# A fused two-block kernel: the delta rule's inverse in 64 by 64 products, the weights' high half first, and a new merged order

## The chip, the cores and the metric

One core of one Trainium2 chip. The metric is the device time of one execution in microseconds (us). The kernel is written instruction by instruction for the five engines: TensorE (PE, its weight loads shown as PEld), VectorE (DVE), ScalarE (ACT), GpSimd (POOL) and SyncE (SP), which only issues transfers.

## The reference, cut to what matters

There are 256 tokens of width 1024. Block one, two layers, mixes sparse attention with a gated delta rule. Block two, two layers, mixes four kinds of attention. All weights are float32 and are read once.

The part that the change rewrites is the delta rule's chunk solve. There are 8 heads, chunks of 64 tokens, and each chunk has a unit lower triangular matrix of 64 by 64:

```python
lower = jnp.where(strict, jnp.einsum('bhnid,bhnjd->bhnij', kb, k) * decay, 0.0)
tmat = jnp.eye(CHUNK) + lower
u = lax.linalg.triangular_solve(tmat, v * beta[..., None], left_side=True, lower=True, unit_diagonal=True)
w = lax.linalg.triangular_solve(tmat, kb * jnp.exp(gc)[..., None], left_side=True, lower=True, unit_diagonal=True)
```

The rest of the work is projections `h @ w_in`, `mixed @ w_out` and their likes in block two, and the attentions.

## The kernel before, in words

**Projections ("mm" steps).** The weights come as 277 units of up to 128 by 1024 float32. SP loads a unit into one of five raw slots. ACT copies it to a float32r high half (step `split`, L1345 by way of L1331). POOL subtracts to get the low half (L849). PE then multiplies in three passes, high by high, high by low, low by high (L916; L902 for the tiles whose stationary operand is the weights; L909 for the narrow ones). Before the first matmul of a unit, PE waits for POOL's low half. Most units are 12 instructions of 512 columns each or 24 of 256.

**The delta rule.** The kernel works on 128 tokens at once (row block r = 0, 1), on four heads at a time (group g = 0, 1), in two layers: four inverses in all. A 128 by 128 lower triangular matrix is inverted: 8 by 8 diagonal blocks first, on DVE (`sub`), then four levels that double the block, 8, 16, 32, 64. `x1` turns the start on PE with transposes. A level n has: `invY`, four products lt by xx on PE (L1014), masked by DVE into yy (L1996); `invZ`, four products xt by yy on PE (L1014), subtracted by DVE from xx (L2003); `invT`, four PE transposes of xx (L937), copied by ACT into xt. The last level is done on the 64-row halves (L1059, L1061 are its two interleaved products; each reads 64 rows and writes 128 partitions). A four-product step is 8 PE instructions (two for each float32 product); a four-transpose step is 4.

**Attention scores on 64-row operands.** `raw` (L1124), `sbz` (L1212) and `sc2` (L1272) hold two heads in the two 64-row halves of a tile. Their loops do the products of the lower rows first, then those of the upper rows.

**Order.** Every engine runs its own instructions in order. The steps come from lanes (a: chains of the delta rule and the like, b: attention, s: splits, m: mm, c, d, v, w: convolution and drains, x, y, e: the ends of layers), and one string, ORDER, says letter by letter which lane goes next. All engines follow this one merged order, so PE does a chain step and then an mm unit and so on, and a chain's latency on DVE and ACT lies behind mm units. Two PSUM tiles of 4 KB a partition ("chain") are taken in turn by chain steps; two others ("bulk") by the projections.

In the merged order of before, PE's steps around the inverse of layer 1, group 0, read (g.r.n): x10.0 x10.1 invY0.0.0 invY0.1.0 invZ0.0.0 invZ0.1.0 vT0 invY0.0.1 mm26 invT0.0.0 invY0.1.1 invT0.1.0 mm27 mm28 iT0 invZ0.0.1 invZ0.1.1 invY0.0.2 invT0.0.1 mm29 and so on.

Of the kernel before, what the change touches and what calls it, by code (L numbers as in the profile page):

```python
# [25 lines left out]
ALU = mybir.AluOpType  # L26
# [3 lines left out]
P = 128  # L30
S = 256
# [22 lines left out]
K_ID, K_TRIU, K_LEVEL, K_BLOCK, K_NEG, K_STR, K_NSTR, K_TRIL, K_ONE, K_FREQ, K_UNIT, K_LATER, K_HALF = (  # L54
    0, 128, 256, 768, 896, 1152, 1408, 1664, 1792, 1920, 1960, 1968, 2096)
K_COLS = K_HALF + 1


def shape_constants():
# [5 lines left out]
    for n, s in enumerate(LEVELS):  # L65
        c[:, K_LEVEL + n * P:K_LEVEL + (n + 1) * P] = (
            (p // (2 * s) == f // (2 * s)) & (p // s % 2 == 1) & (f // s % 2 == 0))
    c[:, K_BLOCK:K_BLOCK + P] = p // BLK == f // BLK
    c[:, K_UNIT:K_UNIT + BLK] = p % BLK == np.arange(BLK)[None, :]
# [162 lines left out]
def gdn_chain(g):  # L232
# [3 lines left out]
    for n in range(len(LEVELS)):  # L236
        for r in range(R):
            if n < len(LEVELS) - 1 or not r:
                out.append(("invY", g, r, n))
            if n:  # L240
                out.append(("invT", g, r, n - 1))
# [59 lines left out]
def lanes():  # L301
# [20 lines left out]
    "aaaaasamsmvasmsmasassasmaaaacmamscsccascmmsaccaasmmcssmasammcscscmmaasdasbamabmasamsaammmsasabsmmaas"  # L322
    "dmaamcsbaaaasmaaasaadmsaasmasdmaaaasaaamaabamaamssacbmsamsacsmcamsbscacsmcmsbascmmcbcmscsascambmbmab"
    "sbaasmsasaaamabdassmmbsmmsmacmdabsdsmaasmaamaawassbdbabmsmamaxmsxsbbbmwamabsabxbasamasaaasbaababamaa"
    "dsdsbamawswmsmbsammamabsdsaamsmwsxdaxmasxxxbswsmxxbbxammsxsvssmvsmmaaaasmmsssmmmamamsvdmaasmassmssmm"
    "acaacmssmccscamcsacsmamsmcsasaccmmmsamsassacamamascsaamsdammssmmammmadssaabsaasbaaaamabsaamdmsbaasaa"
    "maabadaaaaamaaabsssmabmabamaamcsscascmscsabcmmascmmscsbcmcmsscasmcmabmabsaasdmsaaasbmaasbmasmmsdbmam"
    "sambmscamasssaaaaaamdbsaawmxsasmbbbamsdbmbmabssamaxbbmbbsmssdbbmwwammsabasdaaamsxaamdwaawamamsxsabsm"
    "sasbxsamadawbabxxmxmxsssxmxxsmsvsmsmvsmmsamaammaasasmassammmsmsmdsmmssdsabsmmsmdssdssmmbmmmasmsbasas"
    "amamsbbdadammmabssabsdmbmbabbvamsassdabbmasmbsambbssmmbddasbmdmsbbsmbsbsymamyabdysmsabdvmasbyysmdbds"  # L330
    "yysvvdssdmmymsvvvvmmmmmssvmmdvvvvssymsmsmvvsssyvvsmmvvmsmmmemsmemsmsevvmvvaeamesmmeaamsmmmssmmassmms"
    "dmmsssdmsmbdmamssbaasssadasbamsmammmmbabbdsbbsmsammbbdsabamdabbmbavmssbasmbsabmbymsdmbasmbdsdssaambb"
    "mmbasmyysbdsdmssayvmbsmdydbymyvvssmdysmmsvvmdssssvvvmmmdvvsmmsvvysvvsmmsmymssmvvmmsvvemmeemvvmvvmmme"
    "ee"
# [3 lines left out]
def plan():  # L338
# [17 lines left out]
    "kk": "vector", "rep": "vector", "x1": "scalar", "kT": "vector", "invY": "vector", "invZ": "vector", "invT": "scalar", "vT": "vector",  # L356
# [105 lines left out]
def build(nc, t, out):  # L462
    ctx = ExitStack()
    with ctx:
# [62 lines left out]
        kd, st = xx[:, 0, :, :], xx[:, 1, :, :]  # L527
        xt = area(R, 4, P)
        yy = area(R, 4, P)
        rhs = xx[:, 0, :, :].rearrange("p j n -> p (j n)")  # L530
# [160 lines left out]
        def bank_order(i, per):  # L691

            return 2 * (i % (per // 2)) + i // (per // 2)

# [162 lines left out]
        def _(pe):  # L857
            def handlers(p):
# [15 lines left out]
                def mm(u, half=None):  # L874
# [16 lines left out]
                    pe.wait_ge(*p.after("gpsimd", "split", u))  # L891
# [3 lines left out]
                    for k in range(nk):  # L895
                        kk = k0 + k
                        if w["lhs"] == "T":
                            for j in range(4):
                                dst = pair[:, j * S:(j + 1) * S]
                                a_hi, a_lo = hi[:, k, j * P:(j + 1) * P], lo[:, k, j * P:(j + 1) * P]  # L900
                                for i, (a, b) in enumerate(((a_hi, hT_hi), (a_hi, hT_lo), (a_lo, hT_hi))):
                                    m = pe.matmul(dst, a, b[:, kk, :], start=(kk == 0 and i == 0 and j % 2 == 0),  # L902
                                                  stop=(kk == tot - 1 and i == 2 and j % 2 == 1),
                                                  skip_group_check=True)
                        elif w["lhs"] == "narrow":
                            if p.sec == "one" and kk % 4 == 0:
                                pe.wait_ge(*p.after("vector", "hT", kk // 4))
                            for i, (a, b) in enumerate(((hi, hT_hi), (hi, hT_lo), (lo, hT_hi))):
                                m = pe.matmul(pair[0:n, 0:S], a[:, k, :], b[:, kk, :], start=(kk == 0 and i == 0),  # L909
                                              stop=(kk == tot - 1 and i == 2))  # L910
                        else:
                            for r in range(R) if half is None else (half,):
                                dst = pair[:, r * 512:r * 512 + n]
                                a_hi, a_lo = lhs(w, kk, r)
                                for i, (a, b) in enumerate(((a_hi, hi), (a_hi, lo), (a_lo, hi))):
                                    m = pe.matmul(dst, a, b[:, k, :], start=(first and k == 0 and i == 0),  # L916
                                                  stop=(last and k == nk - 1 and i == 2))
# [16 lines left out]
                def transposes(c, srcs, n=P):  # L934

                    for i, v in enumerate(srcs):
                        m = pe.transpose(c[0:n, i * P:i * P + v.shape[0]], v, ident[0:v.shape[0], 0:v.shape[0]])  # L937
                    return m
# [105 lines left out]
                def invY(g, r, n):  # L1044
# [3 lines left out]
                    else:  # L1048
                        pe.wait_ge(*p.after("vector", "invZ", g, r, n - 1))
                    if n < len(LEVELS) - 1:  # L1050
                        four(c, [(lt[:, r, j, :], xx[:, r, j, :]) for j in range(4)]).then_inc(p.done("invY"), 1)
                    elif r == 0:
                        four(c, [(lt[0:P // 2, r, j, :], xx[0:P // 2, r, j, :]) for j in range(4)]).then_inc(p.done("invY"), 1)
                    else:
                        pe.wait_ge(*p.after("vector", "invY", g, 0, n))
                        pe.wait_ge(*p.after("scalar", "invT", g, 0, n - 1))
                        low, up = slice(0, P // 2), slice(P // 2, P)
                        for j in range(4):
                            pe.matmul(c[:, j * P:(j + 1) * P], yy[up, 0, j, :], xt[up, 0, j, :], start=(j == 0), stop=(j == 3),  # L1059
                                      skip_group_check=True)  # L1060
# [1393 lines left out]
```

## Time and profile before

| | us |
|---|---|
| runs | 1102.52, 1100.67, 1099.73 |
| median | 1100.67 |
| profiled execution, first to last instruction (span) | 1099.5 |
| PE busy | 1057.8 (96% of the span) |
| POOL / DVE / ACT busy | 661.4 / 633.4 / 589.4 |
| mean granted TensorE clock | 0.992 |

Three runs stand beside one profiled execution, for which the span is the only time given. "Busy" is time in which an engine has at least one instruction in flight; a matmul's shown duration includes the pipeline's latency, so the cost of a matmul in a stream is the distance from its start to the next one's start, not its duration.

### The profile page before, as it was taken

What the parts mean: (1) busy time and instruction counts of PE and PEld (TensorE: products, weight loads), DVE (VectorE), ACT (ScalarE), POOL (GpSimd) and SP (SyncE); (2) the same over time, 40 slices, a digit from 0 to 9 for tenths busy, and PEclk for the clock granted to TensorE, in tenths of its full rate; (3) what the DMA queues carried; (4) which work ended last, traced back from release to release, by engine and by line L of the source; (5) the groups of instructions that cost most, each with busy time, mean ns of one, the idle gap of its engine ahead of it and who ended that gap; (6) DMA issues with size and microseconds to landing.
All of it is one profiled execution on the core that took longest, in us unless ns stands there. A gap on an engine that the chain in (4) does not pass through costs nothing.

```text
span 1099.5 us, 16938 instructions
## 1 busy us (share of the span) xinstructions
PE 1057.8 (96%) x6368; PEld 916.2 (83%) x6368; DVE 633.4 (58%) x1193; ACT 589.4 (54%) x994; POOL 661.4 (60%) x286
## 2 busy tenths in 40 slices
PE   8999999999989999999999998999999899999986
PEld 8988898888877998889888887788888677898865
DVE  4777358786475547547578465506436650655564
ACT  3753347554644485336756644355577534557652
POOL 4775455854546777525755554697454877645493
PEclk9999999999999999999999998999999999999998
DMA  8644334434234555314444333474332556433361
GB/s 284 205 154 134 97 116 135 154 116 153 96 98 127 190 167 161 118 56 136 141 147 134 97 116 96 137 244 143 116 106 86 194 151 210 129 94 117 110 200 49
DMA packets 80575, 151.60 MB, mean 138 GB/s; under 512 B 6448, under 2 KB 12400, under 8 KB 80496
## 3 DMA queue, kind: packets, MB, share of 16 engines
q1 hardware_dynamic: 80496, 150.54, 42.9%
q8 instruction: 51, 0.84, 0.3%
q14 instruction: 28, 0.23, 0.1%
HBM read 149.47 MB, written 1.05 MB: 137 GB/s over the span
## 4 chain that ended last, share of the span: by engine, by line
PE 84%; DVE 6%; ACT 3%; POOL 3%; issue 3%; DMA 0%; POOLq 0%; SPq 0%; DVEq 0%; ACTq 0%
PE bulk L916 49%; PE bulk L902 11%; PE chain L1014 8%; PE chain L937 6%; POOL w_lo L849 2%; PE chain L1291 1%; PE chain L1272 1%; PE chain L1144 1%; PE bulk L909 1%; PE chain L1160 1%; ACT w_hi L1331 1%; DVE arena L1730 1%; ACT arena L1331 1%; PE chain L1005 1%; PE chain L1124 1%
## 5 line engine op out<-in xcount | busy, mean ns | idle before, releaser
L849 POOL TENSOR_TENSOR w_lo<-raw,w_hi 128x1024 fp32r<-128x1024 f32 (+4 forms) x277 | 647.0, 2349 | 416.7 <-ACT w_hi L1331 416.1
L1331 ACT ACTIVATE w_hi<-raw 128x1024 fp32r<-128x1024 f32 (+4 forms) x277 | 279.5, 1019 | 187.3 <-PE bulk L916 157.8
L916 PE MATMUL bulk<-w_hi,hT_hi 128*128 128x512 f32 (+1 forms) x756 | 307.0, 406 | 10.4 <-POOL w_lo L849 5.8
L916 PE MATMUL bulk<-w_hi,hT_lo 128*128 128x512 f32 (+1 forms) x756 | 295.3, 391 | 0.0
L916 PE MATMUL bulk<-w_lo,hT_hi 128*128 128x512 f32 (+1 forms) x756 | 295.0, 390 | 0.0
L916 PEld LDWEIGHTS bulk<-w_hi,hT_hi 128*128 128x128 f32 x756 | 142.9, 189 | 44.9 <-issue 10.1
L916 PEld LDWEIGHTS bulk<-w_hi,hT_lo 128*128 128x128 f32 x756 | 142.6, 189 | 29.9
L916 PEld LDWEIGHTS bulk<-w_lo,hT_hi 128*128 128x128 f32 x756 | 143.0, 189 | 26.0 <-issue 1.0
L1331 ACT ACTIVATE arena<-chain 128x512 f32<-128x512 f32 (+4 forms) x92 | 62.0, 686 | 118.1 <-PE chain L937 88.5
L902 PE MATMUL bulk<-hT_hi,w_hi 128*128 128x256 f32 x384 | 111.2, 290 | 0.0
L902 PE MATMUL bulk<-hT_hi,w_lo 128*128 128x256 f32 x384 | 108.7, 283 | 0.0
L902 PE MATMUL bulk<-hT_lo,w_hi 128*128 128x256 f32 x384 | 108.6, 283 | 0.0
L1014 PE MATMUL chain<-arena 128*128 128x128 f32 (+1 forms) x800 | 105.3, 279 | 3.0 <-DVE arena L2003 0.8
L1014 PEld LDWEIGHTS chain<-arena 128*128 128x128 f32 (+1 forms) x800 | 98.1, 191 | 10.8 <-DVE arena L2003 1.9
L937 PE MATMUL chain<-cst,arena 128*128 128x128 f32 (+3 forms) x672 | 92.5, 275 | 3.9 <-DVE sT_lo L1675 1.4
L937 PEld LDWEIGHTS chain<-cst,arena 128*128 128x128 f32 (+3 forms) x672 | 76.8, 141 | 15.1 <-DVE sT_lo L1675 1.6
L902 PEld LDWEIGHTS bulk<-hT_hi,w_hi 128*128 128x128 f32 x384 | 73.6, 192 | 1.2 <-issue 0.8
L1838 DVE SCALAR_TENSOR_TENSOR arena<-bulk,par,arena 128x253 f32<-128x253 f32 (+2 forms) x144 | 59.4, 474 | 25.8 <-ACT arena L1331 24.5
L902 PEld LDWEIGHTS bulk<-hT_lo,w_hi 128*128 128x128 f32 x384 | 73.6, 192 | 0.0
L902 PEld LDWEIGHTS bulk<-hT_hi,w_lo 128*128 128x128 f32 x384 | 73.5, 191 | 0.0
L1331 ACT ACTIVATE arena<-bulk 128x1024 f32<-128x1024 f32 (+2 forms) x50 | 50.3, 1006 | 35.3 <-PE bulk L916 35.1
L1326 ACT ACT_TABLE_LOAD x40 | 51.3, 1283 | 24.5 <-PE bulk L916 8.1
(259 smaller groups left out, 1331.4 us busy)
## 6 DMA issues: line engine op xcount, KB each, us to landing
raw<-in_w_in_dram SPq DMA_DIRECT2D x194, 512.0 KB, 3.4
raw<-in_w_out_dram SPq DMA_DIRECT2D x32, 512.0 KB, 3.5
raw<-in_w_branch_dram SPq DMA_DIRECT2D x16, 512.0 KB, 3.6
raw<-in_w_mem_kv_dram SPq DMA_DIRECT2D x8, 512.0 KB, 3.7
raw<-in_w_merge_up_dram SPq DMA_DIRECT2D x16, 256.0 KB, 2.7
raw<-in_w_in_dram SPq DMA_DIRECT2D x8, 420.0 KB, 3.2
gain<-in_ln_rows_dram SPq DMA_DIRECT2D x4, 512.0 KB, 5.1
gain<-in_gains_dram SPq DMA_DIRECT2D x3, 512.0 KB, 5.9
```

Of the source, the lines that this page charges most:

```text
L849: pool.tensor_tensor(lo_of(p, u)[:, 0:n], raw_of(p, u)[:, 0:n], hi_of(p, u)[:, 0:n].bitcast(F32), ALU.subtract).then_inc(p.done("split"), 1)
L902: m = pe.matmul(dst, a, b[:, kk, :], start=(kk == 0 and i == 0 and j % 2 == 0), stop=(kk == tot - 1 and i == 2 and j % 2 == 1), skip_group ...
L909: m = pe.matmul(pair[0:n, 0:S], a[:, k, :], b[:, kk, :], start=(kk == 0 and i == 0), stop=(kk == tot - 1 and i == 2))
L916: m = pe.matmul(dst, a, b[:, k, :], start=(first and k == 0 and i == 0), stop=(last and k == nk - 1 and i == 2))
L937: m = pe.transpose(c[0:n, i * P:i * P + v.shape[0]], v, ident[0:v.shape[0], 0:v.shape[0]])
L1005: pe.matmul(c[:, j * P:(j + 1) * P], spread(4 * g + j, 8), gcT[:, r * P:(r + 1) * P], start=(j == 0), stop=(j == 3), skip_group_check=True)
L1014: m = pe.matmul(c[:, j * P:(j + 1) * P], a, b, start=(j == 0), stop=(j == 3), skip_group_check=True)
L1124: m = pe.matmul(c[:, i * nk:(i + 1) * nk], qiT[lo_:lo_ + 64, h // 2, qb * P:(qb + 1) * P], kiT[lo_:lo_ + 64, 0:nk], start=(i * nk % 512 == 0),
L1144: m = pe.matmul(c[:, j * nk:(j + 1) * nk], qaT[:, 4 * kv + j, qb * P:(qb + 1) * P], kaT[:, kv, 0:nk], start=(j * nk % 512 == 0), stop=((j ...
L1326: act.preload_act_table_set(sets[func])
L1331: return act.activation(dst, src, func, **more)
L1838: ins = STT(cv[:, j, back:S], b[:, j * S:(j + 1) * S - back], par1[:, p.l, c:c + 1], cv[:, j, back:S], ALU.mult, ALU.add)
```

## The change

Five parts.

1. The inverse works on compact halves. The two 64 by 64 diagonal blocks of a 128 by 128 matrix stand in partitions 0 to 63 and 64 to 127 of a tile of 64 columns. A level is now products of 64 rows by 64 columns by 64 columns, two to a head, one in each diagonal quadrant, alternating (`half_blocks`). `invZ` makes both Z and its transpose (operands swapped) in one step, so `invT` is gone from PE and ACT; DVE subtracts both, each of 128 by 256 elements where it subtracted one of 128 by 512. `x1` becomes products with the identity. The last level writes only the 64 partitions that it needs.
2. An mm unit does all passes that need the weights' high half first, waiting only for ACT; then it waits for POOL and does the passes of the low half. The instructions are the same in number and shape.
3. `raw`, `sbz`, `sc2` take their products in the order 0, n/2, 1, n/2+1, ..., so lower-row and upper-row products alternate (`bank_turns`).
4. ORDER is new, without the 24 `invT` steps. Around the inverse of layer 1, group 0, PE's steps now read: x10.0 x10.1 mm24 invY0.0.0 mm25 invY0.1.0 invZ0.0.0 invZ0.1.0 mm26 vT0 invY0.0.1 mm27 iT0 iT1 mm28 invY0.1.1 invZ0.0.1 invZ0.1.1 invY0.0.2 invY0.1.2 invZ0.0.2 invZ0.1.2 invY0.0.3 mm29 invY0.1.3 kT0 mm30 invZ0.1.3.
5. The level masks in the constants are 64 columns wide, and the constants 1841 columns, from 2097.

```diff
+        xh, yh, xth = xx[:, :, :, 0:HALF], yy[:, :, :, 0:HALF], yy[:, :, :, HALF:P]
...
+        def bank_turns(per):
+
+            return [i for pair in zip(range(per // 2), range(per // 2, per)) for i in pair]
...
-                    pe.wait_ge(*p.after("gpsimd", "split", u))
...
+                    pe.wait_ge(*p.after("scalar", "split", u))
+                    for low in (False, True):
+                        if low:
+                            pe.wait_ge(*p.after("gpsimd", "split", u))
+                        part = lo if low else hi
+                        for k in range(nk):
...
+                                for r in range(R) if half is None else (half,):
+                                    dst = pair[:, r * 512:r * 512 + n]
+                                    a_hi, a_lo = lhs(w, kk, r)
+                                    for i, a in enumerate((a_hi,) if low else (a_hi, a_lo)):
+                                        m = pe.matmul(dst, a, part[:, k, :], start=(first and not low and k == 0 and i == 0),
+                                                      stop=(last and low and k == nk - 1))
...
+                def half_blocks(c, pair, col=0):
+
+                    for j in range(4):
+                        for at in halves:
+                            a, b = pair(j, at)
+                            m = pe.matmul(c[at, col + j * HALF:col + (j + 1) * HALF], a, b, start=(j == 0), stop=(j == 3),
+                                          skip_group_check=True)
+                    return m
...
-                    transposes(c, [xt[:, r, j, :] for j in range(4)]).then_inc(p.done("x1"), 1)
+                    half_blocks(c, lambda j, at: (xth[at, r, j, :], ident[at, at])).then_inc(p.done("x1"), 1)
...
-                        four(c, [(lt[:, r, j, :], xx[:, r, j, :]) for j in range(4)]).then_inc(p.done("invY"), 1)
+                        half_blocks(c, lambda j, at: (lt[at, r, j, at], xh[at, r, j, :])).then_inc(p.done("invY"), 1)
...
-                        four(c, [(xt[:, r, j, :], yy[:, r, j, :]) for j in range(4)]).then_inc(p.done("invZ"), 1)
+                        half_blocks(c, lambda j, at: (xth[at, r, j, :], yh[at, r, j, :]))
+                        half_blocks(c, lambda j, at: (yh[at, r, j, :], xth[at, r, j, :]), 512).then_inc(p.done("invZ"), 1)
...
-                def invT(g, r, n):
-                    c = take("invT", g, r, n)
-                    pe.wait_ge(*p.after("vector", "invZ", g, r, n))
-                    transposes(c, [xx[:, r, j, :] for j in range(4)]).then_inc(p.done("invT"), 1)
...
-                    for i in range(per):
+                    for i in bank_turns(per):
```

## Rows read from the trace of the kernel before

**Rows 1.** The page: PE's busy time, and the chain that ended last.
```profile
PE 1057.8 (96%) x6368; PEld 916.2 (83%) x6368; DVE 633.4 (58%) x1193; ACT 589.4 (54%) x994; POOL 661.4 (60%) x286
...
PE 84%; DVE 6%; ACT 3%; POOL 3%; issue 3%; DMA 0%; POOLq 0%; SPq 0%; DVEq 0%; ACTq 0%
PE bulk L916 49%; PE bulk L902 11%; PE chain L1014 8%; PE chain L937 6%; POOL w_lo L849 2%; PE chain L1291 1%; PE chain L1272 1%; PE chain L1144 1%; PE bulk L909 1%; PE chain L1160 1%; ACT w_hi L1331 1%; DVE arena L1730 1%; ACT arena L1331 1%; PE chain L1005 1%; PE chain L1124 1%
```

**Rows 2.** Waits of PE: total us, times, longest.
```profile
PE bulk L916 <- POOL w_lo L849: 7.6, 11, 1.8
PE bulk L916 <- issue: 5.7, 3, 3.6
...
PE bulk L909 <- POOL w_lo L849: 0.4, 1, 0.4
```

**Rows 3.** Busy time by window: start:end and length, PE, PEld, DVE, ACT, POOL, clock, DMA.
```profile
600.00:708.00 108.00, 101.65 (x565) 86.43 (x563) 59.75 (x92) 53.84 (x99) 57.33 (x23) 0.97 0.37 117
```

**Rows 4.** Groups of PE instructions by line: busy us, mean ns.
```profile
L1014 PE MATMUL chain<-arena 128*128 128x128 f32 (+1 forms) x800 | 105.3, 279 | 3.0 <-DVE arena L2003 0.8 <-DVE arena L1996 0.8 <-DVE arena L2023 0.7
L937 PE MATMUL chain<-cst,arena 128*128 128x128 f32 (+3 forms) x672 | 92.5, 275 | 3.9 <-DVE sT_lo L1675 1.4 <-DVE arena L1992 0.8 <-DVE arena L1996 0.4
```

**Rows 5.** The chain that ended last, in order of time: start us, length us.
```profile
96.53 1.79 PE chain L1014 x16
98.31 2.79 PE bulk L916 x12
...
116.30 0.44 PE chain L937 x4
```

**Rows 6.** Timeline of PE, 127.5 to 129.5 us: start us, length us.
```profile
127.53 0.66 PE L937 MATMUL chain<-cst,arena 128*128 128x128 f32 x4 [0.27 <-DVE arena L1992]
128.11 0.37 PE L1059 MATMUL chain<-arena 64*128 64x128 f32 x1
128.12 0.37 PE L1061 MATMUL chain<-arena 64*128 64x128 f32 x1
128.33 0.27 PE L1059 MATMUL chain<-arena 64*128 64x128 f32 x1
...
129.21 0.39 PE L902 MATMUL bulk<-hT_hi,w_hi 128*128 128x256 f32 x1
129.43 0.28 PE L902 MATMUL bulk<-hT_lo,w_hi 128*128 128x256 f32 x1
```

**Rows 7.** Weight loads of 8 and of 128 columns: min/median/max ns.
```profile
L987 PEld LDWEIGHTS chain<-cst,tiny x8: 87/90/91, 34.2 to 392.6; 128*8 128x8 f32 x8
...
L971 PEld LDWEIGHTS chain<-tiny,cst x8: 186/192/193, 30.3 to 383.2; 128*128 128x128 f32 x8
```

**Rows 8.** Timeline of PE at 802 us: 64 moving columns, 128 weight columns.
```profile
802.00 1.00 PE L1291 MATMUL chain<-arena 128*128 128x64 f32 x8
802.84 1.04 PE L937 MATMUL chain<-cst,arena 128*128 128x128 f32 x8
```

**Rows 9.** Timeline of weight loads after an idle wait of PE, 65.5 us.
```profile
65.55 0.18 PEld L1005 LDWEIGHTS chain<-cw_rows,cst 8*128 8x128 f32 x1 [0.80 <-issue]
65.59 0.18 PEld L1007 LDWEIGHTS chain<-arena,cst 8*128 8x128 f32 x1
```

**Rows 10.** DVE and ACT instructions around the inverse: min/median/max ns.
```profile
L1996 DVE TENSOR_TENSOR arena<-chain,cst x24: 690/692/693, 98.1 to 627.0; 128x512 f32<-128x512 f32 x24
...
L1331 ACT ACTIVATE arena<-chain x92: 267/597/1028, 65.2 to 1033.2; 128x512 f32<-128x512 f32 x58, 128x1024 f32<-128x1024 f32 x22, 8x128 f32<-8x128 f32 x4, 128x128 f32<-128x128 f32 x4
```

**Rows 11.** Timeline of PE: the steps raw, 16 and 8 instructions.
```profile
143.96 1.71 PE L1124 MATMUL chain<-arena 64*128 64x128 f32 x16
145.60 0.39 PE L902 MATMUL bulk<-hT_hi,w_hi 128*128 128x256 f32 x1
...
159.96 1.14 PE L1124 MATMUL chain<-arena 64*128 64x256 f32 x8
```

**Rows 12.** POOL's low half of the weights: min/median/max ns.
```profile
L849 POOL TENSOR_TENSOR w_lo<-raw,w_hi x277: 1012/2396/3382, 13.2 to 1080.3; 128x1024 fp32r<-128x1024 f32 x124, 128x512 fp32r<-128x512 f32 x8, 128x840 fp32r<-128x840 f32 x4, 128x704 fp32r<-128x704 f32 x1
```

More of the change, by code:

```diff
@@ L239, in gdn_chain @@
                 out.append(("invY", g, r, n))
-            if n:
-                out.append(("invT", g, r, n - 1))
         if n == len(LEVELS) - 1:
@@ L327 @@
[L327 to L331, printed above, removed]
@@ L894, in mm @@
                     lo = lo_of(p, u)[:, 0:nk * n].rearrange("p (k n) -> p k n", k=nk)
[L895 to L917, printed above, removed]
@@ new lines, in mm @@
+                    pe.wait_ge(*p.after("scalar", "split", u))
[4 more added lines that the diff above has]
+                        for k in range(nk):
+                            kk = k0 + k
+                            if w["lhs"] == "T":
+                                for j in range(4):
+                                    dst = pair[:, j * S:(j + 1) * S]
+                                    for i, b in enumerate((hT_hi,) if low else (hT_hi, hT_lo)):
+                                        m = pe.matmul(dst, part[:, k, j * P:(j + 1) * P], b[:, kk, :],
+                                                      start=(not low and kk == 0 and i == 0 and j % 2 == 0),
+                                                      stop=(low and kk == tot - 1 and j % 2 == 1),
+                                                      skip_group_check=True)
+                            elif w["lhs"] == "narrow":
+                                if p.sec == "one" and kk % 4 == 0 and not low:
+                                    pe.wait_ge(*p.after("vector", "hT", kk // 4))
+                                for i, b in enumerate((hT_hi,) if low else (hT_hi, hT_lo)):
+                                    m = pe.matmul(pair[0:n, 0:S], part[:, k, :], b[:, kk, :], start=(not low and kk == 0 and i == 0),
+                                                  stop=(low and kk == tot - 1))
+                            else:
+                                for r in range(R) if half is None else (half,):
[4 more added lines that the diff above has]
+                                                      stop=(last and low and k == nk - 1))
@@ L1209, in sbz @@
                     n = S - k * P
-                    for q in range(4):
+                    for q in bank_turns(4):
                         h = head_of(1, q)
@@ L1269, in sc2 @@
                     nk = keys_of(n, qb)
-                    for q in range(4):
+                    for q in bank_turns(4):
                         h = head_of(n, q)
@@ L1309, in handlers @@
                             p2T=p2T, pv2=pv2, yT=yT, gT=gT, mm=mm, memT=memT, hT=hT, cwT=cwT, gc=gc_, stat=stat, gcT=gcT_, avT=avT_, dec=dec, kk=kk, rep=rep, x1=x1, kT=kT, vT=vT,
-                            invY=invY, invZ=invZ, invT=invT, kq=kq, u=u_, st=st_, ks=ks, o=o_, iT=iT, raw=raw_, qT=qT, kaT=kaT_,
+                            invY=invY, invZ=invZ, kq=kq, u=u_, st=st_, ks=ks, o=o_, iT=iT, raw=raw_, qT=qT, kaT=kaT_,
                             sc=sc, pT=pT, pv=pv, mT=mT)
```

102 lines of the change are left out of this document (57 added, 45 removed).

## The prediction

> **What bounds the kernel now.** I read the page first [rows 1]: PE is busy for 1057.8 of 1099.5 us, and the chain that ended last lies on PE for 84%. The waits of PE [rows 2] are small and spread; the clock [rows 3] falls only where a layer ends, and there PE idles 6 us of 108. So the time is the sum of what PE has to do plus some 40 us of idle time, and an edit counts by the PE time that it takes away, unless it opens a wait. DVE, ACT and POOL are busy for under 61%; work taken from them counts only through PE's waits.
>
> Durations on PE include latency, so I cost by start-to-start distance. Two L1014 steps, 16 instructions, last 1.79 us and an mm unit 2.79 [rows 5]: 0.112 us for one of the two instructions of a float32 product of 128 by 128 by 128. Four transposes take 0.44, 0.109 each [rows 5].
>
> **Part 1, the inverse: what goes.** For one layer and group, x1 has 8 transposes; invY and invZ at three levels and two row blocks have 96 instructions; invT has 24 transposes; the last level has 8, 16 interleaved and 8. That is 32 x 0.109 = 3.5, 96 x 0.112 = 10.8, and for the last level 0.9 + 0.9 + 0.9 = 2.7 us, since the 16 interleaved run as 8 pairs, both of a pair within 0.01 us, 0.112 a pair [rows 6]. Sum 16.9, and 67.7 us for the four inverses. It is all on PE's path (448 of the 800 and 128 of the 672 instructions of [rows 4]; the rest of them stay; L1059 and L1061 hold 64 more).
>
> **What comes.** Each half_blocks call is 16 instructions, 8 pairs. There are 20 calls (x1 2, invY 6, invZ 12), and the last level has 8 single, 8 pairs, 8 single: 184 places for one layer and group, 736 in all. The unknown is the time p of a place with 64 weight columns and 64 moving ones. Bounds:
> - Low, 0.056. A weight load of 8 columns shows 90 ns and one of 128 shows 192 [rows 7], so 64 columns cost about 0.054 less than 128; half of 0.112 is 0.056. 736 places are 41.2 us.
> - High with pairing, 0.112: L1291 moves only 64 columns under 128 weight columns, and its 8 instructions still take 0.84 to the next start and so give no gain [rows 8]. I read that as the weight load being the limit, which the change halves too; were it not, 736 places are 82.4 us.
> - Between: after an idle wait one load and its matmul reach PE each 0.04 us [rows 9], so a pair (two of each) would be fed at 0.072 to 0.08. While an mm unit runs, the queue is fed ahead, and most inverse steps stand behind an mm unit.
>
> I take 0.060, near the low end since both rows that vary the columns say that time follows them: 44.2 us. The step saves 67.7 - 44.2 = **23.5 us**.
>
> All this counts on the two quadrants running side by side. The one place of before in which two row halves overlap writes two PSUM banks [rows 6]; half_blocks writes one bank, in different partitions. The Trainium skill, TensorEngine Tiling (Array Packing), PSUM Pressure, says that different row tiles cannot use one PSUM bank at the same time; its page PSUM — Partial Sum Buffer, on bank collisions, narrows this to one bank within the same partitions, which the diagonal quadrants do not share. No run here shows which holds. By the first page the quadrants go one by one and the sum is that of the first rival, 1115; by the second it is my forecast, 1082.
>
> **What it costs: changes of shape.** Where PE goes from 128-row work to 64-row work and back, it loses time. In [rows 6] the last transpose starts at 127.53 + 0.66 - 0.27 = 127.91 and the first 64-row matmul 0.20 later, where 0.11 would do; from 128.11 to the second L902 matmul at 129.43 are 1.32 us, of which 8 x 0.112 + 0.12 = 1.02 are work. So a visit costs 0.09 + 0.30 = 0.39 us. From the two merged orders I count the visits (neighbouring steps of one shape are one visit): before 34, after 23 of the 64-row kind and 38 of the quadrant kind, 61. 27 more x 0.39 = **+10.5 us**. I price the quadrant visit like the 64-row visit, which is the nearest row; half as much would give +3, half as much again +18.
>
> **DVE and ACT.** invY's DVE instruction falls from 0.69 us to about half; invZ has two of half size in place of one; ACT's invT copies, 24 of about 0.6, go [rows 10]. All of it lies beside PE: 0. It shortens the chain's latency, and the chain needs this: the new order has a run of eight inverse steps without an mm unit (layer 1, group 0), each waiting on DVE's answer to the one before last. There PE's own 0.5 to 1 us a step covers about that of DVE and the semaphores. I put +1 for it, between 0 and +4.
>
> **Part 2, high half first.** PE's waits for POOL are 7.6 + 0.4 us in 12 places, the longest 1.8; the "issue" waits are 5.7 in three, of which the longest is 3.6, so the other two are 1.0 each, and I read them as the same wait [rows 2]. With 8 of 12 matmuls ahead of the second wait, POOL may come 8 x 0.227 = 1.8 us later. Where POOL was late once, the wait goes whole. Where units follow each other, POOL's 2.4 us and its start behind ACT [rows 12] stand against PE's 2.73, so POOL keeps up. I take **-5 us**, between 0 and -9. Late next is ACT's copy, which needs a free slot and has one. The added wait is met in time nearly everywhere; in streams of units a met wait shows no gap (12 instructions in 2.79 [rows 5]), so it costs 0.
>
> **Part 3, alternating.** raw with 128 keys, 16 instructions, takes 1.64 to the next start; of 8 pairs 0.9 and latency remain 1.1, as in [rows 6]. It occurs twice: **-1.1 us**. The 8-instruction form of 256 columns lasts 1.14 [rows 11]; one by one it would be 8 x 0.22, so it is paired already: 0. The same holds for sbz and sc2.
>
> **Parts 4 and 5.** The order moves waits around. The two large chain lines idle 3.0 and 3.9 us in all [rows 4], part of it at the layers' ends, which stay. I put 0, between -4 and +4. Narrower masks load fewer bytes behind other loads: 0.
>
> **Sum**: -23.5 + 10.5 + 1 - 5 - 1.1 = -18.1. Against the profiled execution's span, 1099.5, this gives 1081.4; the median of the runs is 1.2 above that span, so 1082.6, say **1082**.
>
> **Rivals.**
> 1. *Quadrants go one by one* (slower). Place: every half_blocks call. Then 344 places for each inverse, 1376 x 0.056 = 77.1 us in place of 67.7: +9.4 + 10.5 + 1 - 5 - 1.1 = +14.8, so 1115. For it: both quadrants write one bank, where the pairs of [rows 6] write two, and no row shows 64 weight columns. Against it: the pairs of [rows 6] overlap although both write all 128 partitions; here the two share neither rows, nor columns, nor partitions. It decides from p = 0.085 upward (736p = 62.6, where the sum is nil). Chance 0.11, the case of p = 0.112 for other causes included.
> 2. *The feed limits* (p = 0.072 to 0.08, 53 to 59 us): -18.1 + 8.8 to 14.7, so 1091 to 1097. For it: the quadrant steps are 32 short instructions with the waits between them, and [rows 9]. Against it: the mm unit ahead gives 2.7 us to queue them. Chance 0.16.
> 3. *The change of shape eats it*: with 61 visits at 0.6 us and the eight-step run with real stalls, the gain is about zero, 1098 to 1103. Part 2 then may give nothing too, since POOL sets the pace of the last mm units and the wait only moves. Chance 0.08.
> 4. *My forecast*, 1072 to 1090: chance 0.65.
>
> **Numbers.** A measurement of this kernel tells about 0.3%, 3.3 us, from no change. Faster: all of 4, nearly all of 2: 0.80. Same: 0.09, from 3 and the edge of 2. Slower: 0.11. The range: the low end takes p = 0.056 (-3), all of part 2 (-4), a kind order (-4), less the +1: 1070. The high end reaches through rival 2 and into rival 3, 1101; what is left out is rival 1 and the far ends.
>
> **What would show it.** In the changed kernel's timeline, quadrant instructions come in pairs with about 0.06 us from pair to pair; 0.112 for two of them, one after the other, speaks for rival 1. PE's matmul count rises from 6368 by 4 x (352 - 160) = 768 to 7136, its busy time falls to about 1044. L937 falls by 128 instructions. PE's waits on POOL are under 4 us. The first mm matmul after a quadrant step starts 0.2 us after its last instruction, and the second is late by 0.1. The prediction is wrong if the mm units themselves slow, if DVE shows as PE's releaser for more than 10 us, or if the granted clock drops within the inverses.

## The result, and the profile after

The changed kernel takes **1071.26 us** (median of four runs, 1069.61 to 1073.65), the kernel before 1100.35 beside it: a ratio of 0.9727 [0.9708, 0.9746], 29 us faster where 18 were forecast. It lies inside the range, near its low end.

The page of the changed kernel: span, busy times, the chain that ended last.

```profile
span 1071.6 us, 18457 instructions
PE 1035.5 (97%) x7136; PEld 890.8 (83%) x7136; DVE 605.4 (56%) x1225; ACT 577.6 (54%) x972; POOL 665.2 (62%) x286
PE 88%; DVE 7%; ACT 2%; issue 1%; POOL 1%; DMA 0%; SPq 0%; DVEq 0%; ACTq 0%; POOLq 0%
```

PE is still the bound [rows 1]. Its busy time fell by 22.3 us although it runs 768 matmuls more; the span fell by 27.9, so 5.6 us of the gain are idle time.

The waits of PE after, which answer to [rows 2] (line, releaser: us in total, times, longest).

```profile
PE chain L947 <- DVE arena L2226: 3.6, 2, 2.7
PE bulk L926 <- issue: 3.1, 2, 2.0
PE chain L968 <- DMA cst<-in_shape_constants_dram: 2.8, 1, 2.8
PE chain L947 <- DVE arena L1835: 2.5, 1, 2.5
PE bulk L926 <- POOL w_lo L855: 1.2, 2, 0.9
```

The 8.0 us of waits on POOL are 1.2. The lines of PE that answer to [rows 4], and DVE's two that answer to [rows 10] (busy us, mean ns of one, then the idle time before).

```profile
L955 PE MATMUL chain<-arena 64*64 64x64 f32 x1152 | 40.0, 220 | 1.8 <-DVE arena L2008 1.1 <-DVE arena L2018 0.5
L955 PE MATMUL chain<-cst,arena 64*64 64x64 f32 x128 | 4.6, 221 | 0.0
L947 PE MATMUL chain<-cst,arena 128*128 128x128 f32 (+1 forms) x544 | 74.1, 277 | 7.3 <-DVE arena L2226 3.6 <-DVE arena L1835 2.5 <-DVE arena L1760 0.7
```
```profile
L2008 DVE TENSOR_TENSOR arena<-chain,cst 128x256 f32<-128x256 f32 x24 | 10.2, 424 | 41.9 <-PE chain L955 41.5
L2015 DVE TENSOR_TENSOR arena<-arena,chain 128x256 f32<-128x256 f32 x24 | 10.1, 421 | 16.5 <-PE chain L955 16.4
```

The 1280 quadrant instructions of x1 and of the first three levels occupy PE for 44.6 us, and PE waits before them for 1.8 us in all: DVE keeps up.

PE's timeline at x1 (start, length, line, count), two calls and the mm unit behind them:

```profile
90.50 0.84 PE L926 MATMUL bulk<-w_lo,hT_hi 128*128 128x512 f32 x3
91.27 1.15 PE L955 MATMUL chain<-cst,arena 64*64 64x64 f32 x32
92.35 0.50 PE L926 MATMUL bulk<-w_hi,hT_hi 128*128 128x512 f32 x1
92.69 0.39 PE L926 MATMUL bulk<-w_hi,hT_lo 128*128 128x512 f32 x1
```

Instruction by instruction, the 32 start in 16 pairs, both of a pair within 0.01 us; from the first to the last start are 0.93 us: 0.10 to the second pair, then 0.058 from pair to pair. The first mm matmul starts 0.15 after the last pair, the second 0.34 later where 0.227 would do. The other visits agree: 0.93 is the value for 32 instructions (9 visits in all), 1.40 for 48 (4): 8 pairs are 0.467. The mm units did not slow: 120 units of 12 matmuls ahead of block two take 2.60 us from first to last start in both kernels (median).

### The profile page after: what moved, and what is told of

Same layout as the page of the kernel before. It is cut to its first block, busy times and chain, and to the rows that moved or that the text cites. A ratio compares the mean times of both kernels' runs of the same rounds, so it can differ in the third digit from the quotient of the medians.

```text
span 1071.6 us, 18457 instructions
## 1 busy us (share of the span) xinstructions
PE 1035.5 (97%) x7136; PEld 890.8 (83%) x7136; DVE 605.4 (56%) x1225; ACT 577.6 (54%) x972; POOL 665.2 (62%) x286
## 4 chain that ended last, share of the span: by engine, by line
PE 88%; DVE 7%; ACT 2%; issue 1%; POOL 1%; DMA 0%; SPq 0%; DVEq 0%; ACTq 0%; POOLq 0%
PE bulk L926 52%; PE bulk L911 13%; PE chain L947 5%; PE chain L955 4%; PE chain L1033 4%; PE chain L1310 2%; PE chain L1291 1%; PE chain L1179 1%; PE chain L1163 1%; DVE arena L1835 1%; PE chain L1024 1%; PE bulk L919 1%; ACT w_hi L1350 1%; ACT arena L1350 1%; POOL w_lo L855 1%
## 5 line engine op out<-in xcount | busy, mean ns | idle before, releaser
L926 PE MATMUL bulk<-w_lo,hT_hi 128*128 128x512 f32 (+1 forms) x756 | 203.3, 389 | 1.3 <-POOL w_lo L855 1.2
L911 PE MATMUL bulk<-hT_hi,w_hi 128*128 128x256 f32 x384 | 96.2, 289 | 0.0
L911 PE MATMUL bulk<-hT_lo,w_hi 128*128 128x256 f32 x384 | 94.0, 283 | 0.0
L1350 ACT ACTIVATE arena<-chain 128x512 f32<-128x512 f32 (+5 forms) x68 | 46.3, 696 | 74.0 <-PE chain L947 33.2
L947 PE MATMUL chain<-cst,arena 128*128 128x128 f32 (+1 forms) x544 | 74.1, 277 | 7.3 <-DVE arena L2226 3.6
L947 PEld LDWEIGHTS chain<-cst,arena 128*128 128x128 f32 (+1 forms) x544 | 62.8, 142 | 14.9 <-issue 7.9
L911 PE MATMUL bulk<-hT_hi,w_lo 128*128 128x256 f32 x384 | 53.9, 283 | 0.0
L1350 ACT ACTIVATE arena<-arena 128x128 f32<-128x128 f32 (+2 forms) x65 | 37.8, 585 | 26.7 <-DVE arena L1929 16.2
L911 PEld LDWEIGHTS bulk<-hT_hi,w_lo 128*128 128x128 f32 x384 | 49.5, 192 | 0.0
L1350 ACT ACTIVATE arena<-arena,tiny 128x256 f32<-128x256 f32 (+1 forms) x80 | 36.2, 454 | 18.3 <-DVE tiny L2348 16.8
```

What stands on the lines that cost most here:

```text
L911: m = pe.matmul(dst, part[:, k, j * P:(j + 1) * P], b[:, kk, :], start=(not low and kk == 0 and i == 0 and j % 2 == 0), stop=(low and kk = ...
L926: m = pe.matmul(dst, a, part[:, k, :], start=(first and not low and k == 0 and i == 0), stop=(last and low and k == nk - 1))
L1350: return act.activation(dst, src, func, **more)
```

## The granted clock, which the sum had left out

The runs of one kernel differ by their mean granted clock. The changed kernel gave 1073.65 us at 0.991, 1071.35 at 0.995 and 1069.61 at 0.997. In the profiled runs the loss lies in short stretches at the lower of the two levels, 1.2 in place of 2.4 GHz. Windows of the changed kernel (us; busy us and instructions of PE, PEld, DVE, ACT, POOL; granted clock; DMA share; GB/s):

```profile
760.00:762.00 2.00, 1.07 (x10) 1.07 (x10) 1.30 (x2) 1.09 (x5) 0.85 (x1) 1.00 0.09 6
762.00:767.00 5.00, 5.00 (x27) 4.80 (x27) 0.42 (x1) 3.92 (x8) 2.36 (x1) 0.66 0.37 107
1038.00:1042.00 4.00, 1.53 (x9) 1.05 (x8) 3.25 (x3) 0.00 (x0) 4.00 (x2) 1.00 0.57 153
1042.00:1046.00 4.00, 4.00 (x15) 3.28 (x14) 1.23 (x1) 2.92 (x3) 2.65 (x2) 0.57 0.30 113
```

PE had idled in the stretch ahead; then it works without a gap at half clock for part of the next, and a stretch of 5 us at 0.66 loses 1.7 us of work. Four such stretches lie in this execution. So a wait of PE can cost twice: itself, and the clock behind it. It need not. The kernel mix, below, has the same order as the changed kernel at this place and idles there as long; the two lines of the changed kernel, then those of mix:

```profile
646.00:649.00 3.00, 0.52 (x3) 0.10 (x1) 2.87 (x8) 0.00 (x0) 0.00 (x0) 1.00 0.51 167
649.00:654.00 5.00, 4.76 (x18) 4.08 (x19) 1.32 (x2) 2.92 (x3) 1.12 (x1) 0.66 0.00 0
```
```profile
646.00:649.00 3.00, 0.55 (x3) 0.12 (x1) 2.87 (x8) 0.00 (x0) 0.00 (x0) 1.00 0.47 169
649.00:654.00 5.00, 4.75 (x25) 3.99 (x26) 1.33 (x2) 3.59 (x4) 1.48 (x1) 1.00 0.00 0
```

After the same wait the clock fell in one execution and held in the other, and the four runs of the changed kernel itself differ by their clock. So which waits cost twice is at least in part chance.

I take for the loss (1 - clock) x span of each run, and call the run's time less that loss its *time at full clock*. It is a rough account: behind PE's last work the clock is low too and costs nothing, which makes the loss too large by 1.5 to 3.2 us in the profiled executions, so a difference under some 2 us isn't told by it. But the runs of one kernel agree by it: a_wait_front's twelve runs lie within 11.3 us as timed and within 3.3 by it. These are the medians of every kernel that ran; the ratio is of the times as measured, to the kernel before in the same job. The kernels ran in four jobs on different chips, and the kernel before had a median of 1100.35, 1101.10, 1100.19 and 1101.08 us in them, so up to 0.9 us of a difference between kernels of two jobs can be the job.

```
kernel          median us   ratio [95%]               clock   at full clock
before            1101.10   (27 runs of one job)      0.993      1093.5
b_turns           1099.09   0.9980 [0.9966, 0.9993]   0.994      1093.5
b_high            1099.28   0.9986 [0.9975, 0.9998]   0.991      1089.1
b_high_turns      1097.67   0.9968 [0.9958, 0.9979]   0.991      1088.3
a_old_no_high     1087.13   0.9864 [0.9839, 0.9889]   0.991      1077.5
a_order_old       1080.81   0.9819 [0.9801, 0.9836]   0.991      1071.6
a_no_high         1098.23   0.9983 [0.9963, 1.0003]   0.988      1085.7
a_wait_front      1095.93   0.9967 [0.9949, 0.9984]   0.991      1086.2
a_no_turns        1072.10   0.9753 [0.9734, 0.9772]   0.994      1065.7
after             1071.26   0.9727 [0.9708, 0.9746]   0.995      1065.9
a_serial          1084.95   0.9860 [0.9846, 0.9875]   0.994      1078.2
mix               1063.35   0.9654 [0.9632, 0.9677]   0.998      1060.7
v_plain           1082.33   0.9825 [0.9800, 0.9851]   0.994      1075.8
v_quad            1110.66   1.0081 [1.0058, 1.0104]   0.996      1105.7
```

This account was made after the runs; their expectations below don't have it.

## Experiments on high half first and alternating halves

**b_high** is the kernel before with the changed mm unit alone:

```diff
-                    pe.wait_ge(*p.after("gpsimd", "split", u))
-                    for k in range(nk):
+                    pe.wait_ge(*p.after("scalar", "split", u))
+                    for low in (False, True):
+                        if low:
+                            pe.wait_ge(*p.after("gpsimd", "split", u))
+                        for k in range(nk):
...
```

> The kernel before with the high half first alone. My theory: PE's waits on POOL, 8 us in the kernel before, go nearly whole, since 1.8 us of matmuls now stand ahead of the second wait: 5 to 9 us faster, 1091 to 1095, and PE's waits on POOL under 2 us. Rival (POOL sets the pace where units follow each other, the wait only moves into the unit): within 2 us of before, POOL waits stay at 6 us or more.

**Measured:** 1099.28, a gain of 1.8 us; this is the rival's size, not mine. But the waits on POOL did go, as I had it, where the rival had them stay. Waits of PE:

```profile
PE bulk L920 <- issue: 8.4, 3, 3.6
PE chain L953 <- DMA cst<-in_shape_constants_dram: 2.6, 1, 2.6
PE chain L941 <- DVE xs L1749: 2.0, 1, 2.0
```

The one wait on POOL that is left is 0.3 us. The "issue" waits rose from 5.7 to 8.4, two of them from 1.0 to 2.4. The first of the two, in the kernel before and then in b_high:

```profile
873.44 1.23 DVE L2381 TENSOR_TENSOR sT_lo<-chain,sT_hi 128x1024 fp32r<-128x1024 f32 x1
874.77 0.47 PE L916 MATMUL bulk<-w_hi,sT_hi 128*128 128x512 f32 x1 [1.02 <-issue]
```
```profile
872.33 1.23 DVE L2385 TENSOR_TENSOR sT_lo<-chain,sT_hi 128x1024 fp32r<-128x1024 f32 x1
873.66 0.47 PE L920 MATMUL bulk<-w_hi,sT_hi 128*128 128x512 f32 x1 [2.41 <-issue]
```

In both kernels PE starts 0.10 us after DVE's sT_lo, the merged activations' low half, is done. PE is ready for the unit 2.5 us earlier than before, at 871.2 in place of 873.7, and sT_lo comes only 1.1 us earlier. That takes 2.7 of the 7.7 us back. The clock takes most of the rest: behind these two longer waits it falls, where in the kernel before it holds. Windows of b_high, then the same of the kernel before:

```profile
868.00:874.00 6.00, 3.59 (x19) 2.73 (x18) 5.83 (x5) 4.63 (x5) 6.00 (x2) 1.00 0.59 198
874.00:879.00 5.00, 5.00 (x17) 3.92 (x16) 3.85 (x2) 1.09 (x2) 5.00 (x3) 0.66 0.53 165
```
```profile
868.00:874.00 6.00, 5.75 (x30) 4.50 (x28) 5.62 (x5) 2.69 (x4) 5.12 (x3) 1.00 0.56 186
874.00:879.00 5.00, 4.23 (x19) 3.54 (x20) 4.89 (x3) 3.86 (x4) 5.00 (x3) 1.00 0.57 194
```

At full clock b_high gains 4.4 us, close to the -5 of the sum; as timed, 2.6 of them are lost to the clock (medians 0.991 against 0.993).

**b_turns** is the kernel before with the three loops over raw, sbz and sc2 alternating; **b_high_turns** has both.

```diff
-                    for i in range(per):
+                    for i in bank_turns(per):
```

> The kernel before with the alternating row halves alone. My theory: only the two steps raw with 128 keys gain, 0.55 us each, so about 1 us faster, 1099. Rival (the 8-instruction forms gain too, 0.2 us each in a dozen places): 3 to 4 us faster.

> The kernel before with both small parts. My theory: their sum, 6 to 10 us faster, about 1092. What is left to the measured 1071 is then the inverse with its order, about 20 us. Rival (the small parts carry the surplus over my forecast): 1085 or less.

**Measured:** 1099.09, and 1097.67 for both. As timed, alternating gives 2.0 and 1.6 us; at full clock 0 and 0.8. b_turns came out as I had it; for both together I had expected 6 to 10 us and the rival over 16, and 3.4 are neither. In the trace the 16 instructions of raw with 128 keys go from 1.44 us between first and last start to 0.89, while the 8-instruction forms stay (0.77 and 0.76). That is 1.1 us for the two places, as the sum had it. The two steps sbz go from 1.41 to 1.31, which the sum had at nothing. **a_no_turns**, the changed kernel with the plain loops, asks it from the other side:

> The changed kernel with the lower-row products first again. It measured 2 us in the old order. Theory (it is PE work and adds in any order): 1073 to 1074. Rival (the new order covers it): 1071.

**Measured:** 1072.10, 0.8 us more than the changed kernel as timed, 0.2 less at full clock. That is between my 1073 to 1074 and the rival's 1071. In the changed kernel the part is worth nothing that these runs can tell.

## Experiments on the wait, the order of products and the merged order

**a_order_old** is the changed kernel with the merged order of before, less its 24 invT steps. It separates the inverse from the order.

> The changed kernel with the merged order of before, of which only the 24 steps that no longer exist are left out; it has 61 visits to 64-row or quadrant work too. My theory (the order is worth little, the surplus comes from smaller prices): 1068 to 1077. Rival (the new order carries the 11 us by which the change beat my forecast): 1080 to 1085, with PE waits on DVE and ACT several us longer.

**Measured:** 1080.81, so my theory missed and the time is the rival's: the new order is worth 9.5 us as timed, where the sum had 0 with bounds of 4. By the clock account 5.7 are order and 3.8 are clock. Waits of PE:

```profile
PE bulk L926 <- issue: 8.4, 3, 3.6
PE chain L947 <- DVE arena L1760: 2.3, 2, 1.5
PE chain L1080 <- DVE arena L2004: 2.1, 2, 1.0
PE chain L1179 <- ACT arena L1350: 1.9, 1, 1.9
PE chain L1074 <- DVE arena L2018: 1.5, 3, 0.5
```

L1080 and L1074 are the inverse's last level (the second and the first row block of invY), waiting for DVE: the old order leaves too little between steps that now take PE half as long. In the changed kernel L1080 has no such wait and L1074 has 0.5 us. But the rival's reason does not show in the sums: PE waits for DVE and ACT 20.3 us here and 20.2 in the changed kernel, which waits elsewhere. What is longer is "issue", 8.4 against 3.1 us, 4.8 of it the two waits before sT units that b_high has too. All waits are 31.6 against 27.3 us, so of the 5.7 us of order 4.3 are seen as waits. Up to the place where both orders have issued the same 731 steps (just into block two), they are 23.2 against 15.3; behind it they are 8.4 against 12.0, so the new order gains ahead of block two and loses in it.

**a_no_high** is the changed kernel, new order included, with the mm unit of before: POOL's wait at the unit's start, and the three products in the old sequence.

> The changed kernel with the low half waited for at the unit's start again, passes in the old order. In the old order the high half first gave 1.5 us only, since the time it saved was waited for elsewhere. Theory A (it pays with the new order, which puts the steps behind it earlier): 5 us or more slower than the changed kernel, 1076 to 1082. Theory B (it is worth 1 to 2 us in any order): 1072 to 1074.

**Measured:** 1098.23, 27 us more than the changed kernel, where I had expected 5 to 11; nearly the whole gain is gone. Waits of PE on POOL:

```profile
PE bulk L922 <- POOL w_lo L855: 16.1, 15, 2.6
PE bulk L908 <- POOL w_lo L855: 3.8, 3, 1.7
PE bulk L915 <- POOL w_lo L855: 3.2, 2, 2.8
```

23.1 us in 20 places, where the kernel before has 8.0 in 12 [rows 2]. At full clock the part is worth 19.8 us; the other 7 are clock (0.988 against 0.995).

**a_wait_front** tells apart the two things that a_no_high undid: it keeps the changed sequence of products and only moves the wait to the front.

```diff
-                    pe.wait_ge(*p.after("scalar", "split", u))
+                    pe.wait_ge(*p.after("gpsimd", "split", u))
                     for low in (False, True):
-                        if low:
-                            pe.wait_ge(*p.after("gpsimd", "split", u))
```

> The changed kernel with its new order of passes, but waiting for POOL's low half at the unit's start. Theory (only the place of the wait matters, not the order of the passes): the same time as the kernel with the old passes, within 1 us. Rival (the order of the passes changes the rate of the matmuls): between the two, or off by over 2 us.

**Measured:** 1095.93, 2.3 us under a_no_high's 1098.23 where I had expected 1, but with intervals that overlap; at full clock 1086.2 beside 1085.7, the same. Its waits on POOL are nearly the same too, 22.0 us against 23.1:

```profile
PE bulk L924 <- POOL w_lo L855: 16.0, 15, 2.6
PE bulk L917 <- POOL w_lo L855: 3.2, 2, 2.8
PE bulk L909 <- POOL w_lo L855: 2.8, 2, 1.7
```

So it is the place of the wait, not the sequence of the products.

**a_old_no_high** closes the square: old order, quadrants, wait at the front.

> The changed kernel with the order of before and the low half waited for at the unit's start. It completes a square: order old or new, high half first or not. Theory (the new order is built on the high half first, since it puts ACT's and POOL's splits later; the old one is not): 1081 to 1084, so the new order without the high half first (1098) loses some 15 us, and with it wins 9.5. Rival (the high half first is worth 25 us wherever the inverse's quadrants are, since PE is faster now and POOL nearer to the pace): about 1100.

**Measured:** 1087.13, 3 us over my 1081 to 1084 and far from the rival's 1100. The square, as timed and (at full clock):

```
                    wait at the unit's start    high half first
order of before     1087.1 (1077.5)             1080.8 (1071.6)
order of the change 1098.2 (1085.7)             1071.3 (1065.9)
```

The two parts don't add. The new order alone **costs** 11 us (I had expected 15); with high half first it gains 9.5. High half first is worth 6.3 in one order and 27 in the other. In the traces I counted the mm units at which PE's last matmul ahead of the unit had started before POOL had the low half ready. With the high half first they are 28 of 282 with quadrants in the old order (a_order_old) and 57 in the new one (after); with the wait at the unit's start 17 (a_old_no_high) and 32 (a_no_high), and 16 in the kernel before. (POOL makes 277 low halves in w_lo and five in the place of sT and hT, so the units are 282.) The new order runs PE closer behind POOL, and only the later wait makes that nearly free: PE's waits on POOL are 1.2 us after.

**mix** follows the question where the new order gains. Measured by the steps that both orders have issued alike at a place, it is 14.9 us ahead of a_order_old at the 731st step and only 8.3 at the 1048th: it gains in block one and loses in parts of block two. (3.4 of the 14.9 are clock: the low stretches up to there cost 5.1 us in a_order_old and 1.7 in the changed kernel.) mix is the changed kernel with its order up to step 731, that of before to 827, new to 950, old to 1097, new to 1147, old to the end. In short:

```diff
-ORDER = NEW
+ORDER = NEW[:731] + OLD[731:827] + NEW[827:950] + OLD[950:1097] + NEW[1097:1147] + OLD[1147:]
```

> The changed kernel with an order spliced from the two at places where both have issued the same steps: new up to block two, then old, new or old by which of the two was quicker in that stretch of the traces. Theory (the stretches keep their times when spliced): 1060 to 1065, 7 to 11 us faster than the changed kernel. Rival (a stretch is quick at the cost of the next, splits and transfers lent ahead): 1069 to 1073, no better.

**Measured:** 1063.35 (1062.61 to 1064.23), 38 us under the kernel before and 8 under the change, as the theory had it: **the fastest of all**. Two lines of its page:

```profile
span 1061.1 us, 18457 instructions
PE 1028.4 (97%) x7136; PEld 884.1 (83%) x7136; DVE 606.6 (57%) x1225; ACT 576.7 (54%) x972; POOL 664.5 (63%) x286
```

With the same 7136 matmuls PE is busy for 7.1 us less than in the changed kernel: that is mostly the clock, which falls nowhere before the last 4 us (0.998), where PE has no work left; the four stretches of the changed kernel cost 6.8. Its waits sum to 23.6 us against 27.3. By the medians of the runs 2.7 of the 7.9 us are clock and 5.2 are not; of these 3.7 are seen as waits. How much of the clock is the order's doing is open, since at 649 us the two kernels differ in clock with the same order and the same wait. One of its windows, in block two around the place where the change, b_high and a_order_old lose the clock:

```profile
840.00:880.00 40.00, 36.08 (x177) 29.44 (x176) 23.18 (x28) 15.71 (x21) 27.99 (x11) 1.00 0.55 169
```

## Experiments on the quadrants

**a_serial** issues the lower quadrant's four products, then the upper's, where the change alternates.

```diff
-                    for j in range(4):
-                        for at in halves:
+                    for at in halves:
+                        for j in range(4):
```

> The changed kernel with the four products of the lower quadrant first and then the four of the upper one in each half_blocks call. My theory (two quadrants run side by side only when PE sees both within a few instructions): a call of 16 instructions goes from 0.46 us between its first and last start to 0.7 or more, 80 calls: 15 to 28 us slower than the changed kernel, 1086 to 1099. Rival (PE looks far enough ahead to pair them anyway): within 3 us of it.

**Measured:** 1084.95, 13.7 us more (12.3 at full clock), just under the 15 to 28 of the theory. The theory took the difference of one call 80 times; where calls follow each other it is smaller, and over all calls the trace has 52.1 us between first and last starts in place of 39.4, 12.8 more. PE's timeline at the same place as above:

```profile
90.89 1.54 PE L955 MATMUL chain<-cst,arena 64*64 64x64 f32 x32
92.36 0.51 PE L926 MATMUL bulk<-w_hi,hT_hi 128*128 128x512 f32 x1
92.70 0.40 PE L926 MATMUL bulk<-w_hi,hT_lo 128*128 128x512 f32 x1
```

From first to last start of the 32 instructions are 1.32 us in place of 0.93; a call of 16 takes 0.74 in place of 0.46. One by one 16 would take 15 x 0.058 = 0.87, so PE still runs some of the other quadrant's products ahead, but not all. The alternation in half_blocks is part of what makes the change pay.

**v_plain** and **v_quad** measure a visit by itself. v_plain is the changed kernel with 64 more products of identity by identity, 128 by 128, in the narrow tiles of section two; v_quad has a pair of 64 by 64 products before each of them, the first two lines of matmuls below; v_plain has the third alone. Nothing reads these products.

```diff
+                                if p.sec == "two":
+                                    for _ in range(2):
+                                        pe.matmul(pair[0:64, 512:576], ident[0:64, 0:64], ...)
+                                        pe.matmul(pair[64:128, 512:576], ident[64:128, 64:128], ...)
+                                        pe.matmul(pair[:, 512:640], ident, ident, ...)
```

> Control for the price of a visit: the changed kernel with 64 further products of the identity with itself, 128 by 128, in the narrow tiles of block two, in columns that nothing reads. 64 x 0.224: about 14 us over the changed kernel, 1085 to 1087.

> The same with a pair of quadrant products ahead of each of the 64: 4 instructions each, so 64 more visits. By the changed kernel's trace a visit costs 0.29 us and the two pairs 0.116: 64 x 0.41 = 26 us over the control. By my forecast's price, 0.39: 32 us. Were a change of shape free: 7 us.

**Measured:** 1082.33 and 1110.66. v_plain is 11 us over the changed kernel where 14 were expected; 2.2 us of the gap are the two waits of L1259, which the changed kernel has behind the narrow tiles and v_plain has no longer. The difference of the two, 28.3 us over 64 visits (26 were expected by the trace, 32 by the forecast's price), is 0.44 each, less 2 x 0.058 of work 0.33 (0.35 at full clock). One visit in v_quad's timeline of PE:

```profile
752.73 0.28 PE L924 MATMUL bulk<-hT_lo,w_hi 128*128 128x256 f32 x1
752.94 0.27 PE L920 MATMUL bulk<-cst 64*64 64x64 f32 x1
752.95 0.27 PE L921 MATMUL bulk<-cst 64*64 64x64 f32 x1
753.05 0.22 PE L920 MATMUL bulk<-cst 64*64 64x64 f32 x1
753.05 0.22 PE L921 MATMUL bulk<-cst 64*64 64x64 f32 x1
753.20 0.49 PE L922 MATMUL bulk<-cst 128*128 128x128 f32 x2
```

It shows where the price lies: 0.21 from the last 128-row matmul to the quadrants (0.12 in v_plain), 0.10 to the second pair (0.058 in a steady run), 0.15 to the first 128-row matmul (0.058); its successor is late by a further 0.11. That is 0.09 + 0.04 + 0.09 + 0.11 = 0.33. The forecast had 0.39, the price of a 64-row visit.

## Why the prediction was right, and where it was not

The steps along one path, at full clock (us):

```
step                                    forecast   measured   kernels
high half first                           -5         -4.4     before, b_high
alternating                               -1.1       -0.8     b_high, b_high_turns
inverse in quadrants, with its visits    -12.0      -16.7     b_high_turns, a_order_old
new merged order                           0         -5.7     a_order_old, after
clock, as timed less at full clock       not in it   -2.2     before, after
sum                                      -18.1      -29.8     1101.1 to 1071.3
```

(The old order has the visits of the new one, 61, so the third row holds them. The path starts at 1101.1, the kernel before in the job of b_high, and ends in another job; beside its own kernel before the change gains 29.1.)

**The inverse's work** was right: a pair takes 0.058 us where 0.060 was taken, so 736 places are 42.7 and the step saves 25.0 rather than 23.5. L947 fell by 128, the matmuls rose by 768 to 7136, both as written.

**The visits** were sized too high, as the text said they might be, being priced by their nearest row. With 0.33 for the 38 quadrant visits and 0.39 for the 23 of 64 rows they add 12.5 + 9.0 - 13.3 = 8.2 in place of 10.5. With the two corrections the inverse comes to -25.0 + 8.2 + 1 = -15.8, or -16.8 without the +1 for the run of inverse steps; measured -16.7. That it agrees to 0.1 is partly luck: from b_high_turns to a_order_old the span falls by 17.7 us, of which PE's busy time falls by 20.3 and its waits rise by 2.0, among them 3.6 at the inverse's last level that the sum does not have. The signature was right: 0.15 to the first mm matmul (0.2 forecast) and the second late by 0.11.

**The order** is the step that failed, though the total stayed in its range. "I put 0, between -4 and +4" measured -5.7 at full clock and -9.5 as timed, and +8.2 and +11 without high half first. The prediction treated its parts as terms of a sum; these two are one part, since the order decides how often PE meets POOL's wait and the wait's place decides what that costs. The bounds, taken from the idle time of two lines, could not show this. How closely each order runs its units behind POOL might have been estimated in advance from the two orders; this was not tried.

**High half first** was right at full clock and 3 us too high as timed: the sum named what is late next as ACT's copy, and it was DVE's sT_lo before two units, with the clock behind it. Nor were the two "issue" waits of 1.0 us POOL's, as the prediction read them: they ended with sT_lo in the kernel before too, so this part could not remove them. The prediction put the part "between 0 and -9" from the waits of the old order alone; in the new order it is -20, and -27 as timed.

**The clock** stood in the prediction only as a thing that must not fall within the inverses. It did not: the inverses end by 613 us, and the changed kernel's four stretches begin at 650, 762, 872 and 1042. By the account of the table it takes from 2.7 us (mix) to 12.5 (a_no_high), and differs between kernels by as much as several of the terms.

**Alternating** was right in size within what the runs can tell.

**The rivals.** Quadrants one by one: no. Both quadrants write one bank and start within 0.01 us of each other, in every pair. The Trainium skill, TensorEngine Tiling (Array Packing), PSUM Pressure, says that row tiles cannot use one bank at the same time; the trace does not bear this out for quadrants that share no partition, at 0.058 us a pair. The Trainium skill's page PSUM — Partial Sum Buffer, on bank collisions, quotes that broad rule too, but the collision of two row tiles that it reports as measured is narrower, in one bank and the same group of 32 partitions. The diagonal quadrants share none, and the trace agrees. The feed limit: no, 0.058 is under its 0.072. Change of shape: 0.33, not 0.6, and the run of inverse steps hardly stalls: its 176 instructions at 445 us take 5.89 us from first to last start where pairs of 0.058 would take 5.1.

**What was to prove it wrong.** "DVE shows as PE's releaser for more than 10 us" is fulfilled, at 19.3 us, but it was badly set: DVE had 12.5 us before. The larger waits lie outside the inverse (3.6 and 2.5 us before L947 steps). The mm units did not slow (2.60 us before and after). PE's busy time was to be 1044 and is 1035.5; the pairs' and visits' smaller sizes account for 3.8 of the 8.5 us, and the rest was not taken apart.

## What to carry to other kernels

When an instruction stream has one fixed order across engines, the place of a wait and the order are one decision: undo each alone before judging either, since here one alone gained 6 us, the other alone lost 11, and both together gained 16. Before trusting a small gain or loss, compare the granted clock of the runs: behind a wait the clock may fall, at about 1.7 us of PE's work each time, and in another run of the same code it may not. Products that fill a quarter of the array pay if each has its partner issued right beside it and the visits are few: a call of 16 instructions takes 0.46 us against 0.87 one by one, and a visit costs 0.33.

## What the runs showed of the hardware that I had not expected

- A half-clock stretch after PE's idle spells (1.1 to 2.7 us long in the changed kernel) costs about 1.7 us of work each time, and the clock differs from run to run of one kernel: its runs spread by 4 us in the changed kernel (clock 0.991 to 0.997) and by 11 with the wait at the front (0.982 to 0.995). mix, at 0.997 to 0.998, spreads by 1.6.
- PE overlaps quadrants that are issued four and four only in part: 0.74 us for 16 instructions, against 0.46 alternating and 0.87 one by one.
- A quadrant visit is cheaper than a 64-row one: 0.33 against 0.39.
- Halving DVE's instruction from 512 to 256 columns brings it from 0.69 [rows 10] to 0.42 us, not to 0.35.
- Which part of the new order of block two costs time, step by step, was not tried beyond the splice; how much of mix's gain a kernel without these pauses of the clock would keep stays open as well.
